# The end of a 32-expert layer: an expert's weights in halves, the last pieces cut finer, and a scaling moved to GpSimd

## The reference, cut to what matters

```python
def expert_block(args):
    tok, e = args
    xb = xt[tok]
    h = jax.nn.silu(xb @ w_gate[e]) * (xb @ w_up[e])
    return h @ w_down[e]
...
y = y.reshape(n_rows, d) * row_w[:, None].astype(y.dtype)
out = jax.ops.segment_sum(y, row_tok, num_segments=t)
...
return rmsnorm(x, final_g)
```

## Time and profile before

| | us |
|---|---|
| median of 3 runs (lowest, highest) | 1317.46 (1317.33, 1319.31) |
| span of the profiled execution, first to last instruction | 1315.5 |
| median less span: what lies around the span | 1.96 |
| TensorE busy in the span | 1236.0 (94%) |
| VectorE, ScalarE, GpSimd busy | 557.6, 287.5, 6.0 |
| moved by DMA | 471.76 MB, mean 359 GB/s |

### The profile page before, as it was taken

One profiled execution on the slowest core, in us unless ns is written; L12 is line 12 of the kernel. 1 busy time (PEld: TensorE's weight loads), 2 busy tenths in 40 slices (PEclk: granted clock), 3 DMA queues, 4 the chain that ended last, 5 costly groups with the idle time before them and its releaser, 6 DMA issues.

```text
span 1315.5 us, 15712 instructions
## 1 busy us (share of the span) xinstructions
PE 1236.0 (94%) x5942; PEld 647.9 (49%) x5942; DVE 557.6 (42%) x988; ACT 287.5 (22%) x404; POOL 6.0 (0%) x27
## 2 busy tenths in 40 slices
PE   8999999999999999999898989999988999999996
PEld 7888888888874333333333333333333333333332
DVE  6575988774565323232322223223222232232234
ACT  6443454474441011101001000010010000101003
POOL 1000000000000000000000000000000000000000
PEclk9999999999999999999999999999999999999998
DMA  8655454457489999999999999999999999999996
GB/s 306 218 192 182 139 192 166 156 182 298 158 340 345 432 430 430 430 430 431 431 433 431 431 430 431 431 430 431 431 433 431 431 430 431 431 430 431 429 427 265
DMA packets 66129, 471.76 MB, mean 359 GB/s; under 512 B 6151, under 2 KB 6663, under 8 KB 39596
## 3 DMA queue, kind: packets, MB, share of 16 engines
q1 hardware_dynamic: 66092, 471.24, 87.2%
HBM read 469.13 MB, written 2.10 MB: 358 GB/s over the span
## 4 chain that ended last, share of the span: by engine, by line
PE 63%; DMA 31%; DVE 2%; issue 2%; ACT 1%; SPq 0%; DVEq 0%; ACTq 0%
DMA ring<-in_w_up 23%; PE bank L1929 21%; PE bank L1681 10%; PE bank L1689 8%; DMA zone_u<-in_w_up 8%; PE bank L1965 8%; PE bank L1978 5%; PE bank L1690 4%; PE bank L1899 1%; PE bank L1930 1%; DVE zone_u L1089 1%; PE bank L1692 1%; PE bank L2122 1%; DMA x_tok<-in_x 1%; ACT gatesT L885 1%
## 5 line engine op out<-in xcount | busy, mean ns | idle before, releaser
L1929 PE MATMUL bank<-ring,win 128*64 128x512 f32 x816 | 377.3, 617 | 41.4 <-DMA ring<-in_w_up 29.3
L1930 PE MATMUL bank<-ring,win 128*64 128x512 f32 x832 | 380.2, 610 | 0.0
L1929 PEld LDWEIGHTS bank<-ring,win 128*64 128x64 f32 x816 | 112.0, 141 | 284.3 <-issue 265.8
L1689 PE MATMUL bank<-h_both,w_hi 128*128 128x512 f32 x540 | 192.3, 398 | 1.0 <-DVE h_both L1011 0.8
L1461 DVE SCALAR_TENSOR_TENSOR x_tok<-bank,gate_of,x_tok 128x512 f32<-128x512 f32 x248 | 169.1, 744 | 30.3 <-PE bank L1978 29.3
L1965 PE MATMUL bank<-ring,hiddenT 128*64 128x512 f32 x672 | 150.8, 594 | 11.3 <-ACT gatesT L885 11.3
L413 DVE TENSOR_TENSOR w_lo<-stage,w_hi 128x2048 fp32r<-128x2048 f32 x58 | 132.4, 2288 | 64.0 <-ACT w_hi L407 63.9
L1690 PE MATMUL bank<-h_both,w_lo 128*128 128x256 f32 x540 | 151.3, 280 | 0.0
L407 ACT ACTIVATE w_hi<-stage 128x2048 fp32r<-128x2048 f32 x58 | 111.3, 1920 | 121.4 <-PE bank L1690 77.9
L877 ACT ACTIVATE rows_now<-bank,root_row 64x512 f32<-64x512 f32 x31 | 21.1, 681 | 533.1 <-PE bank L1930 533.1
L1978 PE MATMUL bank<-y_rows,gatesT 64*128 64x512 f32 x496 | 123.5, 615 | 0.0
(11 more groups left out here) (274 smaller groups left out, 1055.5 us busy)
## 6 DMA issues: line engine op xcount, KB each, us to landing
ring<-in_w_up SPq DMA_DIRECT2D x49, 2048.0 KB, 31.6
ring<-in_w_gate SPq DMA_DIRECT2D x47, 2048.0 KB, 34.8
ring<-in_w_down SPq DMA_DIRECT2D x41, 2048.0 KB, 31.6
stage<-in_w_in SPq DMA_DIRECT2D x43, 1024.0 KB, 5.0
zone_u<-in_w_down SPq DMA_DIRECT2D x19, 2048.0 KB, 31.7
zone_u<-in_w_up SPq DMA_DIRECT2D x9, 2048.0 KB, 33.6
zone_u<-in_w_gate SPq DMA_DIRECT2D x9, 2048.0 KB, 35.0
stage<-in_w_out SPq DMA_DIRECT2D x16, 1024.0 KB, 5.0
```

Source lines behind the costliest of these rows:

```text
L1689: M.matmul(dst[:, :], hi[:, at], both, start=(c == 0), stop=False)
L1929: M.matmul(dst[0:W_ROWS, :], rows_of[:, c, 0:W_ROWS], gate[:, at], start=(c == 0), stop=(c == C - 1))
L1930: ins = M.matmul(dst[UPPER, :], rows_of[:, c, 0:W_ROWS], up[:, at], start=(c == 0), stop=(c == C - 1))
```

## The change

1. Expert 29 is taken out of the loop and loaded with `load_by_halves` as well; the loop is one round shorter, and experts 27 and 28 are straight code with whole pieces.
2. The last quarter of expert 31's gate and up product is loaded in two parts of 512 KB for each of gate and up (`EIGHTH`), and computed in two steps, each with its own wait. Two scatter matmuls of expert 30 move from behind the third quarter to ahead of it.
3. The right half of expert 31's down weights is loaded and multiplied by quarters of 512 output columns (`last_down(q)`): 256 columns to each half of the partitions, in banks 5 and 0. The third quarter is multiplied ahead of the left half's scatter and scattered right behind it (`scatter_quarter(2)`); then the fourth quarter is multiplied and scattered. A quarter's scatter is four matmuls of 256 columns in two turns; the two turns write the two halves of the same bank and a wait for `crossed` stands between them. ScalarE copies the third quarter to `y_rows`, VectorE the fourth, between its third and its fourth pair of returns.
4. GpSimd makes the products of the left halves with `final_w`, and scales the left half of token block 0 in two parts of 512 columns. ScalarE keeps the left half of token block 1.
5. There are six stores instead of five: token block 0 in four of 512 columns, taken alternately from VectorE and GpSimd, token block 1 in two halves. The crowd code takes over semaphores of the end; it stays unexecuted.

```diff
-ROUNDS = (E - 1) // ROUND
+ROUNDS = (E - 1) // ROUND - 1
+LATE = 3
+NH = NB // 2
...
+        EIGHTH = (slice(PART, PART + PART // 2), slice(PART + PART // 2, PIECE))
-        LAST_BANK = (BACK_BANK, (0, 2, 4, 5))
+        LAST_BANK = (BACK_BANK, (2, 4), (5, 1))
+        DOWN_BANK = (4, 5, 0)
```

On SyncE:

```diff
+            for e in range(ROUNDS * ROUND, E - LATE):
+                src = expert_pieces(e)
+                for k in range(PIECES):
+                    load_next(e, k, slot_of(e, k), src)
...
-            src = expert_pieces(E - 2)
-            load_by_halves(E - 2, src)
-            for k in (down_first, down_last):
-                load_next(E - 2, k, slot_of(E - 2, k), src)
+            for e in range(E - LATE, E - 1):
+                src = expert_pieces(e)
+                load_by_halves(e, src)
+                for k in (down_first, down_last):
+                    load_next(e, k, slot_of(e, k), src)
             src = expert_pieces(E - 1)
             load_by_halves(E - 1, src)
+            for k in (gate_last, up_last):
+                sp.dma_start(ring[slot_of(E - 1, k)][:, EIGHTH[1]], src[k][:, EIGHTH[1]]).then_inc(last_part, 16)
             wait_used(E - 2, 2)
...
+            for k in (down_first, down_last):
+                load_down(k, LEFT, last_loaded[k - down_first])
+            for q in (2, 3):
+                for k in (down_first, down_last):
+                    load_down(k, slice(q * NB, (q + 1) * NB), last_loaded[q])
...
+            for i in range(2):
+                sp.wait_ge(fin_ready, i + 1)
+                store(0, slice(HD + i * NB, HD + (i + 1) * NB), stored)
+                sp.wait_ge(fin_spare, i + 1)
+                store(0, slice(i * NB, (i + 1) * NB), stored)
             sp.wait_ge(fin_left, 1)
             store(1, LEFT, stored)
             sp.wait_ge(fin_ready, 3)
             store(1, RIGHT, stored)
```

On GpSimd:

```diff
+            pool.wait_ge(fg_loaded, 16)
+            for t in range(T):
+                pool.wait_ge(returned, LAST_RETURN + 2 * t + 2)
+                pool.tensor_tensor(left_scaled[:, t, :], x_tok[:, t, LEFT], final_w[:, LEFT], ALU.mult).then_inc(left_made, 1)
+            pool.wait_ge(left_made, 1)
+            pool.wait_ge(fin_scale, 1)
+            for i in range(2):
+                at = slice(i * NB, (i + 1) * NB)
+                pool.tensor_scalar(final_out[:, 0, at], left_scaled[:, 0, at], RSTD[:, 0:1], None, ALU.mult).then_inc(fin_spare, 1)
```

On ScalarE:

```diff
-            last_squares(0, LAST_ORDER[0:2])
-            act.wait_ge(down_used, J * e + J)
-            nc.scalar.activation(y_rows[:, NB:HD], bank[5][:, :], ACT.Copy).then_inc(y_dve, 1)
-            last_squares(0, LAST_ORDER[2:])
-            last_squares(1, LAST_ORDER[0:2])
+            act.wait_ge(down_used, J * e + 3)
+            nc.scalar.activation(y_rows[:, NB:NB + NH], bank[DOWN_BANK[1]][:, 0:NH], ACT.Copy).then_inc(y_third, 1)
+            last_squares(LAST_ORDER)
+            last_squares(THIRD_ORDER)
+            last_squares(FOURTH_ORDER[0:1])
...
             final_root(0)
-            last_squares(1, LAST_ORDER[2:3])
-            final_left(0, slice(0, NB))
-            last_squares(1, LAST_ORDER[3:])
-            final_left(0, slice(NB, HD))
+            last_squares(FOURTH_ORDER[1:])
             final_root(1)
+            act.wait_ge(left_made, 2)
             final_left(1, LEFT)
```

On VectorE:

```diff
-            last_returns(0)
+            last_returns(LAST_BANK[0], LAST_ORDER)
+            last_returns(LAST_BANK[1], THIRD_ORDER)
+            dve.wait_ge(down_used, J * e + J)
+            V.tensor_copy(y_rows[:, NB + NH:HD], bank[DOWN_BANK[2]][:, 0:NH]).then_inc(y_dve, 1)
+            last_returns(LAST_BANK[2], FOURTH_ORDER)
+            final_mean(0)
+            final_scale(0)
             dve.wait_ge(fg_loaded, 16)
-            scale_left(0)
-            scale_left(1)
-            last_returns(1, range(0, 3))
-            final_mean(0)
-            last_returns(1, range(3, 4))
-            final_scale(0)
-            for lo in (HD, HD + NB):
-                scaled_out(0, slice(lo, lo + NB)).then_inc(fin_ready, 1)
+            scaled_out(0, slice(HD, HD + NB)).then_inc(fin_ready, 1)
             final_mean(1)
+            scaled_out(0, slice(HD + NB, D)).then_inc(fin_ready, 1)
             final_scale(1)
             scaled_out(1, RIGHT).then_inc(fin_ready, 1)
```

On TensorE:

```diff
+            def last_down(q):
+                pe.wait_ge(last_loaded[q], 2 * 16)
+                for j in range(J):
+                    weights = piece(E - 1, 5 if j >= 2 else 4)
+                    for tile in range(2):
+                        at = (j % 2) * PART + q * NB + tile * NH
+                        ins = M.matmul(bank[DOWN_BANK[q - 1]][tile * W_ROWS:(tile + 1) * W_ROWS, 0:NH],
+                                       hiddenT[:, j * W_ROWS:(j + 1) * W_ROWS], weights[:, at:at + NH],
+                                       start=(j == 0), stop=(j == J - 1))
+                ins.then_inc(down_used, 1)
...
+            def scatter_quarter(q):
+                y_at = NB + (q - 2) * NH
+                for turn in range(2):
+                    for h in range(T):
+                        tile = (h + turn) % 2
+                        rows_at = UPPER if tile else slice(0, W_ROWS)
+                        M.matmul(bank[LAST_BANK[q - 1][h]][:, tile * NH:(tile + 1) * NH], gatesT[rows_at, h * P:(h + 1) * P],
+                                 y_rows[rows_at, y_at:y_at + NH], start=True, stop=True).then_inc(scattered if turn else crossed, 1)
+                    if turn == 0:
+                        pe.wait_ge(crossed, T * (q - 1))
...
             turn_gates(e)
+            back(e - 1, 1, range(0, 2))
             last_quarter(e, 2)
-            back(e - 1, 1, range(0, 2))
-            last_quarter(e, 3)
+            for i in range(2):
+                pe.wait_ge(last_part if i else last_in[LATE - 1][QUARTERS - 1], 2 * 16)
+                gate_up(e, 3, piece(e, 2), piece(e, 3), win, part=range(2 * i, 2 * i + 2))
             back(e - 1, 1, range(2, 4))
...
-            last_down(1, 0)
+            last_down(2)
             banks_free(E - 1, 0)
-            last_scatter(0)
-            for j in range(1, J):
-                last_down(1, j)
-            last_scatter(1)
+            scatter_left()
+            pe.wait_ge(y_third, 1)
+            scatter_quarter(2)
+            last_down(3)
+            pe.wait_ge(y_dve, E)
+            pe.wait_ge(returned, RETURNS // 2 + RETURNS * (E - 1) + 1)
+            scatter_quarter(3)
```

More of the change, by code:

```diff
@@ L316, in hybrid_moe_program @@
         y_dve = sem("y_dve")
+        y_third = sem("y_third")
+        crossed = sem("crossed")
+        left_made = sem("left_made")
+        fin_spare = sem("fin_spare")
         fg_loaded = sem("fg_loaded")
@@ L596, in _ @@
             with sp.If(flag > 0):
[L597 removed]
+                sp.wait_ge(stored, 16 * STORES)
                 with sp.Fori(E, E + OVER) as t:
@@ L2103, in _ @@
             turn_hidden(e)
-            down(e, piece(e, 4), piece(e, 5), arrived_down(e))
+            down(e, piece(e, 4), piece(e, 5), arrived_down(e, -16))
             def last_turn(z):
```

145 lines of the change are left out of this document (66 added, 79 removed).

## The result

The changed kernel takes **1321.01 us** (median of 8 executions, 1320.88 to 1321.54), the kernel before beside it 1317.59 (8 executions): ratio 1.0024, 95% interval 1.0014 to 1.0033. It is slower by 3.4 us; the forecast was 1317.7 with a range from 1316.0 to 1319.7. The profiled span is 1318.4 us, before 1315.5. So the span is 2.9 us longer, and another 0.5 us lies outside it: the eight executions of the changed kernel last 2.40 to 2.51 us longer than their spans; for the kernel before the median of that difference is 1.9 in every round of the experiments.

What follows compares the result with a forecast made beforehand. Full DMA weight stream bounds it until 1287.10, then a chain of engines and the stores. Down product -0.2, block 0 +0.35, small stores +0.05 give +0.2 us: 1317.7 us, range 1316.0 to 1319.7.

Steps and rivals of the forecast that it cites:

- Straight code: Experts 27 and 28 leaving the loop: no cost, since experts 30 and 31 as straight code show no stall of their own.
- rival D: The clock falls in one of the new stalls ahead of expert 31, costing 1.6 us: 1319.3; chance 0.05.
- GpSimd's scaling: Block 0's left half on GpSimd: two operations of 512 columns, 0.5 to 1.05 us each, done at 1308.5 and 1309.5, in time.
- Rival A: At block 0's scaling VectorE and GpSimd hold each other up, 0.4 to 1.3 us: 1318.6; chance 0.20.
- The queue of stores: SyncE waits in order, so a late GpSimd piece holds back every later store; judged in time, no term in the sum.
- The small stores: Block 0's four 256 KB stores at 381 GB/s, 0.69 us each: +0.05 us; bounds +0.45 and -0.3.
- The time outside the span: Measured median lies 1.96 us above the profiled span; kept unchanged for the forecast.
- Block 0: Mean of token block 0 at 1306.6, 0.47 us later than before, behind the late fourth scatter.
- rival C: 256-column matmuls of the last down product take 0.70 of the long ones: +1.3 us, 1319.0; chance 0.12.
- Rival B: The tail gains two fewer returns behind the last scatter, 1.4 us, and loses nothing more: 1316.3; chance 0.20.
- E: Faster: the 4.1 us won at expert 29 reach the end, needing a stream that was not full: 1313.6; chance 0.04.
- F: Slower: GpSimd's left scaling becomes the bound, at 6.3 us an operation the end comes 5.6 us later: 1323.3; chance 0.03.

Runs made afterwards that it cites:

- e2: The changed kernel with the store of GpSimd's second piece issued last, behind both stores of block 1: 1319.78 us, kernel before 1317.68.
- e1: The changed kernel with ScalarE again scaling the left half of block 0, GpSimd keeping only the products: 1319.93 us, kernel before 1318.14.
- e13: The changed kernel with the ten-round loop kept, expert 29 whole in it, and ScalarE scaling block 0's left columns: 1318.88 us, kernel before 1318.12.
- e9: The kernel before with the last quarter in two parts, the moved scatters and GpSimd's left products: 1317.84 us, kernel before 1318.12.
- e4: The kernel before with only GpSimd's products and scalings and the six stores in changed order: 1319.31 us, kernel before 1318.14.
- e15: The kernel before with 4,096 already met waits added on GpSimd: 1317.71 us, kernel before 1317.68.

## Why the prediction was wrong

- **Straight code, counted as nothing.** This step failed. "Experts 30 and 31 already are straight code and show no stall of their own, so nothing" took two experts behind a loop for a proof about three more. Expert 30's first quarter came as forecast (1243.2 + 0.14; measured 1243.28), its second 1.15 us late (1248.24; 1249.39). The stall of 2.46 us took the clock down with it: 0.83 in the 10 us from 1248, 1.7 us, as for the stall ahead of expert 29 in the earlier trace rows. That is rival D's event, in a stall that I had put at 1 us, but not its price, for the late bytes hold expert 31 anyway. In e2, the changed kernel but for the order of its last stores, the clock stays up there:
```profile
1248.00:1258.00 10.00, 8.31 (x38) 2.87 (x40) 3.15 (x5) 0.00 (x0) 0.00 (x0) 1.00 1.02 430
```
and TensorE waits for expert 31:
```profile
1274.13 0.61 PE L1945 MATMUL bank<-ring,win 128*64 128x512 f32 x1 [1.08 <-DMA ring<-in_w_up]
```
That is 83.95 us behind its expert 28; with the low clock it is 84.25, so the clock is worth some 0.3 us. Expert 31 started at 1273.83 in place of 1272.76. The last quarter in two parts hid a little of it: down product at 1293.54 in place of 1292.7. Worth 1.2 to 1.4 us alone in the runs, 1.0 within the change. Why straight code does it is open.
- **GpSimd's scaling, mis-sized.** The term was 0.5 to 1.05 us each, from a row of another operation, one of two inputs; measured 2.04 and 2.50, of which 1.56 is the operation itself. GpSimd's products, 2.3 us each where 2.1 were forecast, were hidden as said. Rival A named the right pair of engines, but for 0.4 to 1.3 us and with a cover that wasn't there.
- **The queue of stores, put at nothing.** "A late `fin_spare` holds back every later store" was the right mechanism, and the sum had no term for it. With GpSimd's last piece at 1313.02 the remaining 1.3 MB start at 1313.05 and need 3.3 us at 0.39 MB a us, behind 0.9 from issue to flow: 1317.3, where the window from 1317 falls to a share of 0.25. Scaling and queue together are the 1.6 us between the changed kernel and e1.
- **The small stores, mis-sized.** The term was 0.05, from the rate of the earlier trace rows, with +0.45 as the bound from above. In the changed kernel that rate held at first (260 KB at a share of 0.67, 240 at 0.61); in e13, where the four stores follow each other without a hole, 315 to 350 KB a us cost some 0.3 us.
- **The time outside the span, mis-sized.** "1.96 above that span; I keep that": in the changed kernel it is 2.4 to 2.5, which is 0.5 us of the 3.4. It is spread over the differences above: it grows with GpSimd's products, by 0.4 in e9 and by 0.2 in e4.
- **Block 0.** Its mean was forecast 0.47 later than before (1306.6) with the down product at 1292.7; with it at 1293.54 the same step gives 1307.44, measured 1307.54. Held.
- **Held too:** no stall ahead of expert 29; 256-column matmuls at half the time (eight of them 0.86 us, 1297.00 to 1297.86, against 1.74 for eight of 512 columns, 1293.54 to 1295.28), so rival C fell; ScalarE's copy hidden; the fourth scatter behind VectorE's copy (0.53 us of wait). Rival B did not come about, E neither: the stream was full, and what was gained at expert 29 was handed back. F was right that GpSimd becomes the bound and wrong about which operation.
- **A reading that was wrong without harm:** the piece that lands at 1218.63 is expert 29's first up piece, not its last; the count of fourteen pieces to 1287.10 starts from it rightly.

## What to carry to other kernels

Price an operation on an engine by a row of that operation on that engine, format and operand included; where there is none, the bound from above must be wide enough to reach the place at which its consumer is queued in order. At the end of a kernel add up the output's bytes first: when the stores fill the DMA engines, the first store's start and any hole behind it set the end, so a slow producer belongs at the end of the store queue (1.3 us here, e2). Taking experts out of a loop under a full weight stream is a change of its own; measure it alone.

## What the runs showed of the hardware

- Three or six experts as straight code on TensorE delayed the end of a full 427 GB/s stream by 1.2 to 1.6 us, without changing its mean rate measurably. With three the delay arose within 6 us at expert 30, with six from expert 27 on. The cause is not known.
- A 16 KB fetch of code took 0.93 us of one DMA engine (2.9% of 16 over 2 us). TensorE's straight code brought one about every 30 us. GpSimd's code came in blocks of 8 KB, one every 11.4 us while it ran through waits (e15), so no fetch far ahead of its use is shown.
- GpSimd: 128 x 512 f32 by a value for each partition 1.56 us, by a constant 1.49, product of two tensors 1.26 (1,024 columns: 2.36). Started behind a VectorE operation with two inputs in SBUF, the first took 2.04 and 2.50; started ahead of one, 1.56 (e4).
- A wait that is met already is not free on TensorE: 384 of them at the start made the kernel 16.0 us longer, 192 made it 6.2 longer. On GpSimd 4,096 of them took 182 us, from 33.6 to 215.7 (e15).
